# Both feed-forward stages of a decoder step by one level of Strassen, with the sums of weight quarters on VectorE in the up half

## The reference

```python
def conv_ffn(h, prev, w_up, conv_w, conv_b, w_down):
    l = h.shape[1]
    u = h @ w_up
    ext = jnp.concatenate([prev, u], axis=1)
    y = conv_b + sum(conv_w[k] * ext[:, k:k + l] for k in range(CONV_WIDTH))
    a, v = jnp.split(y, 2, axis=-1)
    return (jax.nn.silu(a) * v) @ w_down, ext[:, -(CONV_WIDTH - 1):]
...
        f_p, c_p = conv_ffn(rmsnorm(yp, g_ffn[i]), jnp.zeros((bp, CONV_WIDTH - 1, 2 * D_FF), yp.dtype),
                            w_up[i], conv_w[i], conv_b[i], w_down[i])
        f_s, c_s = conv_ffn(rmsnorm(ys, g_ffn[i]), state_ffn_conv[i], w_up[i], conv_w[i], conv_b[i], w_down[i])
        yp = yp + f_p
        ys = ys + f_s
```

## Time and profile before

| | us |
|---|---|
| median of 3 runs | 3037.19 |
| lowest and highest | 3033.56, 3038.42 |
| profiled execution, its span | 3038.0 |
| TensorE busy | 2935.1 (97%) |
| VectorE busy | 1574.7 (52%) |
| ScalarE busy | 815.3 (27%) |
| GpSimd busy | 966.5 (32%) |
| TensorE's share of the chain that ended last, its last instruction being in the second feed-forward stage | 26% |

### The profile page before, as it was taken

One profiled execution on the slowest core, in us unless ns is written; L12 is line 12 of the kernel. 1 busy time (PEld: TensorE's weight loads), 2 busy tenths in 40 slices (PEclk: granted clock), 3 DMA queues, 4 the chain that ended last, 5 costly groups with the idle time before them and its releaser, 6 DMA issues. The chain is left out here.

```text
span 3038.0 us, 50987 instructions
## 1 busy us (share of the span) xinstructions
PE 2935.1 (97%) x19316; PEld 2715.8 (89%) x19316; DVE 1574.7 (52%) x3486; ACT 815.3 (27%) x1506; POOL 966.5 (32%) x422
## 2 busy tenths in 40 slices
PE   8998989999989999999999999999999999999998
PEld 7996966666767799999999999997999999999998
DVE  6212158888545418744625535495257626436262
ACT  5002037777623304311201111205133202112020
POOL 4430000000000244544444443460435444444443
PEclk9999989999979999999999999999999999999999
DMA  6116740000457311111111111312111111111112
GB/s 186 54 42 227 252 163 2 2 2 2 149 153 228 128 36 60 40 44 49 38 45 49 34 53 37 129 41 115 43 53 42 40 50 45 40 47 41 50 36 91
DMA packets 128683, 222.76 MB, mean 73 GB/s; under 512 B 16118, under 2 KB 92252, under 8 KB 127344
## 3 DMA queue, kind: packets, MB, share of 16 engines
q1 hardware_dynamic: 108548, 201.57, 20.5%
q10 hardware_dynamic: 19980, 19.14, 2.4%
...
## 5 line engine op out<-in xcount | busy, mean ns | idle before, releaser
L382 POOL TENSOR_SCALAR weights_high<-weights_whole 128x1024 fp32r<-128x1024 f32 (+2 forms) x168 | 434.8, 2588 | 1045.8 <-PE banks L417 878.9
L413 PE MATMUL banks<-ffn_in_high,weights_high 128*128 128x364 f32 (+1 forms) x2112 | 467.0, 329 | 9.6 <-DVE ffn_in_low L280 9.6
L415 PE MATMUL banks<-ffn_in_low,weights_high 128*128 128x364 f32 (+1 forms) x2112 | 466.7, 329 | 0.0
L417 PE MATMUL banks<-ffn_in_high,weights_low 128*128 128x364 f32 (+1 forms) x2112 | 465.2, 329 | 0.0
L384 POOL TENSOR_TENSOR weights_low<-weights_whole,weights_high 128x1024 fp32r<-128x1024 f32 (+2 forms) x168 | 375.7, 2236 | 24.7 <-issue 0.2
L2776 DVE SCALAR_TENSOR_TENSOR conv_out<-conv_ext,conv_w,conv_out 128x1024 f32<-128x1024 f32 x176 | 318.7, 1811 | 114.1 <-ACT conv_out L2708 99.7
L413 PEld LDWEIGHTS banks<-ffn_in_high,weights_high 128*128 128x128 f32 x2112 | 366.1, 189 | 11.4 <-issue 11.4
L417 PEld LDWEIGHTS banks<-ffn_in_high,weights_low 128*128 128x128 f32 x2112 | 367.4, 188 | 0.0
L415 PEld LDWEIGHTS banks<-ffn_in_low,weights_high 128*128 128x128 f32 x2112 | 366.9, 189 | 0.0
L2807 DVE TENSOR_TENSOR x<-x,banks 128x728 f32 (+1 forms) x128 | 86.5, 718 | 385.2 <-PE banks L417 385.2
L2708 ACT ACTIVATE conv_out<-conv_ext,conv_b,conv_w 128x1024 f32<-128x1024 f32 (+1 forms) x176 | 138.3, 835 | 536.1 <-DVEq L2767 536.0
...
## 6 DMA issues: line engine op xcount, KB each, us to landing
...
past_rows<-in_kv_pages SPq DMA_DIRECT2D x160, 128.0 KB, 2.4
z<-in_kv_pages SPq DMA_DIRECT2D x96, 128.0 KB, 2.4
...
x<-in_cmp_pages ACTq DMA_DIRECT2D x64, 128.0 KB, 5.8
x<-in_cmp_pages SPq DMA_DIRECT2D x64, 128.0 KB, 5.7
cmp_rows<-in_cmp_pages ACTq DMA_DIRECT2D x64, 128.0 KB, 5.7
```

The source lines that it names most:

```text
L382: pool.tensor_scalar(high, whole, 1.0, None, ALU.mult)
L413: pe.matmul(o, wh, high[:, at], start=kk == 0, stop=False)
L415: pe.matmul(o, wh, low[:, at], start=False, stop=False)
L417: last = pe.matmul(o, wl, high[:, at], start=False, stop=kk == len(terms) - 1)
```

## The change

`conv_ffn` goes, `feed_forward` comes, for both layers. Each product [two output tiles] x [K] x [1088 tokens] is cut in two along all three dimensions: two output tiles, two halves of the chunks of K, two halves of 544 tokens. The eight products of quarters become seven products of sums of quarters (Winograd's form of Strassen's scheme), called blocks 0 to 6. A block of tokens is 544 wide and is multiplied in two pieces of 272 columns, each with its weight load.

**Units.** An up unit q (22 of them) is the pair of output tiles q and q + 22, with four chunks in each half of K: 7 x 4 x 3 x 2 = 168 matmuls. The down half has six parts of 2, 2, 2, 2, 2 and 1 chunks in each half of K (`PAIRS`), each with four units of two output tiles: 7 x 2 x 3 x 2 = 84 matmuls a unit, 42 in the last part.

**Weights.** SyncE loads four quarters for each unit (256 KB each in the up half, 128 KB and 64 KB in the down half) into six slots, each as soon as its slot's last block has been split. Four sums of quarters are made in place: on VectorE in the up half (`first_sums`, `second_sums`), on GpSimd in the first unit and in the down half (`sums`). ScalarE makes the high parts (`round_weights`), GpSimd the low parts (`lower`), in a ring of four blocks: block n is rounded when block n - 4 has been multiplied.

**Products.** Three sets of two PSUM banks of a unit take the seven products; V1, V2, V5 are partial products that ScalarE copies into SBUF, and C11, C22, C12, C21 the quarters of the result: VectorE adds a copy to the bank for the first three (`place`), ScalarE copies the last. Then `edges` (states and tails), the taps, silu and the gate as before. Because tokens are now summed before the product, the norm is applied to them first: squares, their sum, root, spread over partitions, product with `x`, then seven blocks of tokens with high and low parts.

**Between the halves.** The gated values go out to a buffer in HBM (`gated_dram`) and come back part by part as `staged` (2 x 2 x 128 x 1088 values); VectorE makes four differences of them (`gated_sum`, L3049) and the low parts (`lower_gated`, L3110), ScalarE the high parts. In the down half VectorE adds every product to `x` straight out of PSUM (`add`, L3123); no copies. TensorE's product j in a unit waits for the read of the product two before it, for most j.

The project stages ahead no longer split the first up tile on GpSimd (`part_following=False`).

The core of the new code:

```diff
-PARTS = (6, 6, 5, 5)
...
+TH = TE // 2
...
+BLOCKS = 7
+RING = 4
+QUARTERS = 6
+PAIRS = (2, 2, 2, 2, 2, 1)
...
+        LAST_BLOCK = (2, 5, 4, 6)
...
+        UP_ORDER = (0, 0, 0, 0, 1, 5, 2, 6, 3, 4)
+        DOWN_ORDER = (0, 1, 5, 2, 3, 4, 6)
...
+            def stage(p):
+                if p == 0:
+                    sp.wait_ge(multiplied, BLOCKS * (FC - 1) + 1)
+                    sp.wait_ge(gated_stored, 16 * 4)
+                elif p == 1:
+                    sp.wait_ge(gated_stored, 16 * FC)
+                else:
+                    sp.wait_ge(d_split, BLOCKS * p)
...
+            for q in range(1, UNITS):
+                for piece in range(4):
+                    i = 4 * q + piece
+                    if i >= QUARTERS:
+                        q0, p0 = (i - QUARTERS) // 4, (i - QUARTERS) % 4
+                        sp.wait_ge(w_split, BLOCKS * q0 + LAST_BLOCK[p0] + 1)
+                        if p0 == 0 and 0 < q0 < FC:
+                            sp.wait_ge(w_summed_dve, 4 * q0)
+                    sp.dma_start(quarter(q, piece), source(q, piece)).then_inc(q_loaded[i % QUARTERS], 16)
+                    if q == FC and piece == 2:
+                        stage(0)
+                if q == FC + 2:
+                    sp.dma_start(k.outs["conv"][layer], tails[:]).then_inc(stored, 16)
+                    stage(1)
+                elif q > FC + 2 and (q - FC) % PER == 0 and part_of(q) + 1 < len(PAIRS):
+                    stage(part_of(q) + 1)
...
+            def lower(q, j):
+                high, low = ring(q, j)
+                pool.wait_ge(w_rounded, BLOCKS * q + j + 1)
+                pool.tensor_tensor(low, block_source(q, j), high.bitcast(F32), ALU.subtract).then_inc(w_split, 1)
...
+            for q in range(UNITS):
+                if 0 < q < FC:
+                    lower(q, 0)
+                    lower(q, 1)
+                else:
+                    sums(q)
+                lower(q, 2)
+                lower(q, 3)
+                if q == 0:
...
+                    pool.tensor_tensor(n12, n12, over_half(rstd[:, TH:TE]), ALU.mult).then_inc(pool_normed, 1)
+                    high, low = up_block(4)
+                    pool.wait_ge(rounded, len(UP_ORDER))
+                    pool.tensor_tensor(low, up_quadrant(4), high.bitcast(F32), ALU.subtract).then_inc(last_split, 1)
+                for j in range(4, BLOCKS):
+                    lower(q, j)
...
+            def product(q, j):
+                n = width(q)
+                pe.wait_ge(w_split, BLOCKS * q + j + 1)
+                which = "ABAEAEA"[j]
+                wait_read(pe, *((q - 2, "C12"), (q - 1, "C21"), (q, "V1"), (q - 1, "C11"), (q, "V2"), (q, "V5"), (q, "C22"))[j])
...
+                for kk in range(n):
...
+                    for z, (a, b) in enumerate(((wh, high), (wh, low), (wl, high))):
+                        for piece in range(2):
+                            last = pe.matmul(out[:, piece, :], a[:, at], b[:, kk, piece * HP:(piece + 1) * HP],
...
+            for q in range(FC):
+                for j in range(BLOCKS):
+                    if j == 0:
+                        copy(q, "V1")
+                    elif j == 2:
+                        copy(q, "V2")
+                    elif j == 3:
+                        copy(q, "V5")
+                    elif j == 6:
+                        last_quadrant(q)
+                    round_weights(BLOCKS * q + j + RING)
+                    if j == 0 and q:
+                        silu(q - 1)
+                    elif j == 2 and q:
+                        store(q - 1)
+                    elif j == 5:
+                        tap(q, 0)
+                    elif j == 6:
+                        tap(q, 1)
...
+            for q in range(FC):
+                place(q, "C11")
+                place(q, "C22")
+                if q < FC - 1:
+                    first_sums(q + 1)
...
+                place(q, "C12")
...
+                    second_sums(q + 1)
+                    for av in range(2):
+                        edges(q, av)
+                        convolve(q, av, 1)
+                        convolve(q, av, 0)
+                    gate(q)
```

649 lines of the change are left out of this document (443 added, 206 removed).

## The result

| | before | after |
|---|---|---|
| median | 3036.9 us (3033.6 to 3038.4) | 3155.8 us (3153.7 to 3160.7) |
| ratio, 95% interval | 1 | 1.040 (1.038 to 1.041) |
| span of the profiled execution | 3038.0 us | 3158.9 us |

The account below looks back on a forecast made before the run. The prediction took TensorE's matmul stream to bound the kernel before. Start 75, up units 466 and down half 300 make 841 us a stage, 41 more than 800; twice, 82, on 3038 gives 3120 us, range 2975 to 3200.

Parts of the forecast that it names:

- the 184 us: Both feed-forward stages: TensorE's matmul time was to fall to 1394 us, 184 us less, all the change can give.
- Rival 1: Whole kernel: TensorE stays the bound, other engines fit in its shadow; 770 us a stage, 2978 us; chance 0.24.
- its condition: Hand-overs between GpSimd and VectorE under 3 us an up unit, down part at 42.3; sign: no wait for V5.
- rival 3: All matmuls: the weight load, not the columns, sets the pace; 0.166 us a matmul, some 3400 us; chance 0.01.
- the start, 75 us: Start of a stage and first up unit: norm factor, VectorE's preparation and first products take 75 us, bounds 65 and 85.
- the wait that I named: Stage start: TensorE's product 3 stands until VectorE's chain of preparation ends, at 59.5 us.
- An up unit, 22.2 us: Each of 21 later up units takes 22.2 us, between TensorE's own 21.1 and 23.6; 466 us together.
- the ring: Up unit: gate, V5 copy, product 5, add of C12, sums, edges, taps, gate; 15.8 us, 22.2 with GpSimd and waits.
- The taps of 2.4 us: Up units: convolution taps lengthened to 2.4 us beside GpSimd's lower parts, a sign that the forecast is right.
- Part 0, 84 us: First part of the down half, the worst: 42.3 us for TensorE plus delays of 10, 21, 8 and 3, 84 us.
- the lateness of 10: Down part 0: VectorE reaches sums, edges and lower parts for block 2 some 10 us after TensorE wants them.
- The 8 and 3 us behind product 19: Down part 0: late store, part 1's tokens and queued quarter loads, and 11 operations in adds 20 to 27; 8 and 3 us.
- Part 1, 49 us: Second down part, counted like parts 2 and 3: GpSimd's units of 10.6, 14, 13 and 11.4 make 49 us.

Follow-up runs that it names:

- the plain down half: Changed kernel with the down half computed without Strassen, four outputs of 24 matmuls a unit instead of seven products of 12: 3058.4 us, ratio 1.008.

## Why the prediction was right, and where not

**Sign and mechanism.** The forecast's case came: TensorE's stream is no longer the bound, and what the other engines add outweighs the 184 us. Rival 1 was nearer in the steady up half (449 and 450 us, its 443, the forecast's 466), though the wait for the copy of V5 stood there in every unit, against its condition; it failed in the down half. The chance of 0.69 for slower rested on the right places.

**The matmul.** 272 columns at 0.1257 us, worked out from 256: measured 0.125. The same holds in the plain down half, 264.7 us for 2112 matmuls. The weight load, whose record is still 0.19 us, didn't set the pace, so rival 3 is out.

**The step that failed: the start, 75 us.** It measured 96.1 and 97.5. To the norm factor I had 17.5 us; it took 39. I summed TensorE's sum of squares in with the root and the spread at 6 us, as work beside ScalarE's squares. Its 144 instructions last 30.5 us at half clock. The trace of before had the row to price it, in an earlier stage, where 16 f32 matmuls of one column make 32 instructions:

```profile
17.27 1.03 PE L640 MATMUL banks<-ones,mem_squares 128*128 128x1 f32 x8
18.17 1.63 PE L640 MATMUL banks<-ones,z 128*128 128x1 f32 x8
```

The eight of the first row start 0.11 us apart, at the full granted clock; the last of the second stand 0.21 apart, with the clock at 0.51. For 144 that is 16 us or 31, where I had a part of 6. The fourth product started 85.2 and 84.0 us after the stage's start, not 50 to 60.

Behind the factor the sum came near: 57.5 us forecast, 58.3 measured (from the end of ScalarE's copy of the factor, 1174.2, to 1232.5, where the first unit ends). The run with the squares added took 11 us off the first stretch and left the second within 1.3 us of what it was. But the wait that I named, product 3 for its lower part, isn't the one that happened. TensorE stands before product 2, whose lower part VectorE had made by 1207.7; it also needs the copy of V1, which ScalarE makes only behind the rounding of the last two blocks of tokens (the profile names VectorE, whose lower part for product 3 ended at the same time, but product 2 doesn't wait for that):

```profile
1210.14 3.92 ACT L2933 ACTIVATE token_blocks_high<-conv_space 128x2176 fp32r<-128x2176 f32 x2 [2.72 <-DVE token_blocks_low L3044]
1213.97 0.60 ACT L2943 ACTIVATE partial_products<-banks 128x544 f32<-128x544 f32 x1
...
1214.67 0.79 PE L2883 MATMUL banks<-token_blocks_high,weight_blocks_high 128*128 128x272 f32 x2 [16.79 <-DVE token_blocks_low L3044]
```

And product 4 starts at 1223.5, 4.2 us after GpSimd's lower part for it, so it didn't wait for that either. No run moved the copy of V1 ahead of the roundings.

**An up unit, 22.2 us.** Measured 21.4, and the ring ran elsewhere than I had it. The add of C12 never waited: it stands behind VectorE's own two sums, which take 1.7 and 1.6 us beside GpSimd instead of 0.69. What waits is the add of C22, 0.8 us for product 4. From its start to the gate's end are 20.0 us of VectorE without a pause, then 1.5 over the add of C11 and the copy of V5 to the start of product 5; and 21.4 us from product 5 to the add of C22 that the next unit's product 4 releases (seven products of 3.01 and a hand-over). So the ring goes round once in two units: (20.0 + 1.5 + 21.4) / 2 = 21.4. Moving the add and the store out of it gave 21.0. The taps of 2.4 us that I named as a sign did not come in one row: the long instruction stays at 1.30 and the short one reads 1.28 us instead of 0.43 (means of all), which makes a tap 2.6 instead of 1.63. I had five of GpSimd's seven low parts meet a VectorE instruction at 1.2 us each; in the trace all seven do, in the steady units: four short taps, two sums and a copy are each about 1 us longer.

**Part 0, 84 us.** Measured 80, from other terms than I had. The first wait (8.1 us) is the lateness of 10. The steps with lower parts and taps cost 12 (waits before products 3, 4, 6) instead of 21. The 8 and 3 us behind product 19 came out at some 7 (waits before products 21, 23 and 27). What I had left out is the clock: 7.7 us.

**Part 1, 49 us.** Measured 61 to 62.5. I counted it like parts 2 and 3, though its tokens come late, with the sums after adds 23 to 26 and four lower parts after add 27. ScalarE rounds the tokens and the weights in one queue, and waits there for VectorE's sums; GpSimd waits for ScalarE, has three of its own sums to make behind that (1763.8 to 1768.1), and TensorE waits for the low parts that follow:

```profile
1761.15 1.12 ACT L2975 ACTIVATE token_blocks_high<-conv_space 128x1088 fp32r<-128x1088 f32 x1 [4.25 <-DVE conv_space L3049]
1762.65 1.02 POOL L2800 TENSOR_TENSOR weight_blocks_low<-weights_whole,weight_blocks_high 128x256 fp32r<-128x256 f32 x1 [4.94 <-ACT weight_blocks_high L2911]
...
1772.53 0.79 PE L2883 MATMUL banks<-token_blocks_high,weight_blocks_high 128*128 128x272 f32 x2 [6.99 <-POOL weight_blocks_low L2800]
```

I had counted the late operations in part 0 and not what their ScalarE halves do to the weights of part 1. With ScalarE's roundings and VectorE's first seven operations three adds earlier part 1 fell to 50, while part 0 rose by 3; and without GpSimd's sums it fell to 56.

**Parts 2 to 5.** 49, 49, 45, 26.5 against 49.1, 50.2, 43.7, 26.6. Part 2's excess is 6.1 us of waits and 0.9 of half clock. By the waits as shown above, 2.5 us of them are for VectorE's adds (I had 5.2 for its row of seven) and 2.6 for GpSimd's low parts. How the two limits and the token load meet was not in the forecast.

Start +22, up units -16, part 0 -4, part 1 +12, and the 2.5 that I had rounded off: +16 a stage. That is nearly all of the 36 us between forecast and result; the other 3 to 4 lie around the stages. The near hit of the sum hides two terms that were off by more than 10 us and of opposite sign to a third; that they cancel is luck.

**Still open.** GpSimd's exclusion with VectorE is read from lengths and ends of rows, with and without overlap (see below); no run took it apart from everything else. How the 47.3 us without GpSimd's sums divide between VectorE's row and the clock wasn't measured by a run of its own.

## To carry to other kernels

An algorithm that saves matmuls by making sums has to be weighed per stage by what the other engines have free there: the same Strassen step gained 53 us over the 21 steady units of the up half, where VectorE adds three times in 168 matmuls, and lost 46 in the down half, where it adds seven times in 84 and prepares the next part besides. The gain of the up half is not a gain of the stage either: with its start it takes 97.5 + 449.3 = 547 us, against an estimated 538 before (800.5 less 1584 down matmuls of 0.166), because the norm now comes first; only with the start and the ring mended is it 526. Before summing over partitions with TensorE in f32, add the tiles elementwise: the norm factor waited 30.5 us for 72 small matmuls at half clock, and 11 of them came back. In a schedule close to balance, an edit must be followed to where it moves loads and not just to whom it unburdens; and engines that hand work to each other can form a ring over two units, which a reordered add and store may open.

## What the runs showed of the chip

```profile
1381.82 1.30 POOL L2800 TENSOR_TENSOR weight_blocks_low<-weights_whole,weight_blocks_high 128x512 fp32r<-128x512 f32 x1 [2.58 <-ACT weight_blocks_high L2911]
...
1381.89 1.26 DVE L3085 COPY conv_space<-conv_state 128x16 f32<-128x16 f32 x1
```

- After waits of 2 to 8 us, matmuls stand some 0.22 us apart for a while: the granted clock is 0.81 over the 80 us of part 0, where the waits cost 29.7 us and the lower clock 7.7, and 0.81 over the 9 us after a wait of 1.8 us.
- A 128 KB load landed after 2.1 us in the median; its reader started 7.3 and 7.2 us after the issue when two loads of 1088 KB had been issued just ahead of it on the same queue.
